# Splitting the first three units behind each normed phase by token half

## What is computed

```python
h = h + rms_norm(mix, post_mix_g[layer])
f = conv_ffn(rms_norm(h, pre_ffn_g[layer]), ffn_w_up[layer], ffn_conv_w[layer], ffn_conv_b[layer], ffn_w_down[layer])
h = h + rms_norm(f, post_ffn_g[layer])
```

## Time and profile before

| | |
|---|---|
| time, median of 3 runs | 2171.72 us (2171.62 to 2173.23) |
| span of the profiled execution | 2170.2 us |
| TensorE (PE) busy | 2142.6 us, 99% of the span |
| VectorE (DVE) busy | 1434.5 us, 66% |
| ScalarE (ACT) busy | 1015.4 us, 47% |
| DMA, mean over the span | 187 GB/s |
| chain that ended last | TensorE 96%, VectorE 1%, ScalarE 1%, issue 1% |

### The profile page before, as it was taken

The page is one execution under the profiler, slowest core; times in us unless marked ns, Lnnn a source line. Parts: engine busy times, 40 slices in busy tenths (PEclk is TensorE's granted clock), DMA queues, the critical chain, the costliest instruction groups (busy, mean ns, idle before and its releaser), DMA issues.

```text
span 2170.2 us, 32172 instructions
## 1 busy us (share of the span) xinstructions
PE 2142.6 (99%) x11234; PEld 1832.1 (84%) x11234; DVE 1434.5 (66%) x1708; ACT 1015.4 (47%) x1158; POOL 43.9 (2%) x56
## 2 busy tenths in 40 slices
PE   8999999999999999999999999999999999999998
PEld 6888878888888888888788888888888888888887
DVE  5485567878777775444765675567787877774444
ACT  5444454444444444433654574454444444444442
POOL 1030000000000000000000000000000000000000
PEclk9999999999999999999999999999999999999999
DMA  8655546666566666556455544556666666665554
GB/s 269 185 175 174 191 141 202 190 188 191 175 201 190 187 203 199 186 187 209 160 189 189 184 146 165 189 161 194 187 190 183 194 191 186 176 225 194 193 192 152
DMA packets 208226, 406.09 MB, mean 187 GB/s; under 512 B 12496, under 2 KB 12608, under 8 KB 207520
## 3 DMA queue, kind: packets, MB, share of 16 engines
q1 hardware_dynamic: 206784, 398.51, 58.5%
q0 software_dynamic: 1248, 6.67, 0.9%
q10 hardware_dynamic: 128, 0.04, 0.0%
HBM read 403.06 MB, written 2.10 MB: 187 GB/s over the span
## 4 chain that ended last, share of the span: by engine, by line
PE 96%; DVE 1%; ACT 1%; issue 1%; DMA 0%; POOL 0%; DVEq 0%; POOLq 0%; ACTq 0%; SPq 0%
PE ps L1182 37%; PE ps L1185 19%; PE ps L1198 13%; PE ps L1200 12%; PE ps L1199 12%; DVE w_lo L749 1%; PE ps L1253 1%; PE ps L1317 0%; ACT w_hi L441 0%; PE ps L1380 0%; PE ps L1351 0%; ACT x_parts L486 0%; ACT junk L478 0%; DMA h<-in_x 0%; DMA raw<-in_b_w_q 0%
## 5 line engine op out<-in xcount | busy, mean ns | idle before, releaser
L749 DVE TENSOR_TENSOR w_lo<-raw,w_hi 128x1024 fp32r<-128x1024 f32 x752 | 922.9, 1234 | 671.3 <-ACT w_hi L441 666.4
L441 ACT CAST w_hi<-raw 128x1024 fp32r<-128x1024 f32 x752 | 783.8, 1049 | 965.0 <-PE ps L1185 537.7
L1182 PE MATMUL ps<-x_parts,w_hi 128*128 128x512 f32 x3328 | 1161.5, 395 | 4.0 <-issue 2.0
L1185 PE MATMUL ps<-x_parts,w_lo 128*128 128x256 f32 x3328 | 925.2, 278 | 0.0
L1182 PEld LDWEIGHTS ps<-x_parts,w_hi 128*128 128x128 f32 x3328 | 625.7, 188 | 150.9 <-DVE w_lo L749 3.5
L1185 PEld LDWEIGHTS ps<-x_parts,w_lo 128*128 128x128 f32 x3328 | 627.1, 188 | 0.0
L1198 PE MATMUL ps<-w_hi,g_parts 128*128 128x512 f32 x704 | 273.9, 389 | 0.0
L1200 PE MATMUL ps<-w_hi,g_parts 128*128 128x512 f32 x704 | 273.9, 389 | 0.0
L1199 PE MATMUL ps<-w_lo,g_parts 128*128 128x512 f32 x704 | 273.9, 389 | 0.0
L1200 PEld LDWEIGHTS ps<-w_hi,g_parts 128*128 128x128 f32 x704 | 132.1, 188 | 27.7
L1199 PEld LDWEIGHTS ps<-w_lo,g_parts 128*128 128x128 f32 x704 | 132.1, 188 | 27.5
(11 more groups left out here) (147 smaller groups left out, 1505.2 us busy)
## 6 DMA issues: line engine op xcount, KB each, us to landing
raw<-in_ffn_w_up SPq DMA_DIRECT2D x352, 512.0 KB, 3.7
raw<-in_ffn_w_down SPq DMA_DIRECT2D x176, 512.0 KB, 4.3
raw<-in_a_w_in SPq DMA_DIRECT2D x64, 512.0 KB, 4.3
raw<-in_a_w_out SPq DMA_DIRECT2D x32, 512.0 KB, 4.2
raw<-in_b_w_q SPq DMA_DIRECT2D x32, 512.0 KB, 3.6
raw<-in_w_k SPq DMA_DIRECT2D x32, 512.0 KB, 4.1
raw<-in_w_v SPq DMA_DIRECT2D x32, 512.0 KB, 4.1
raw<-in_b_w_o SPq DMA_DIRECT2D x32, 512.0 KB, 4.5
```

Source lines behind the costliest of these rows:

```text
L441: act.copy(w_hi[:, slot, :, :], raw[:, slot, :, :]).then_inc(unit_hi, 1)
L749: dve.tensor_tensor(w_lo[:, slot, :, :], raw[:, slot, :, :], w_hi[:, slot, :, :].bitcast(F32), ALU.subtract).then_inc(unit_split, 1)
L1182: pe.matmul(ps[:, bank + m, :], w_hi[:, slot, kk, m * P:(m + 1) * P], src[:, kt, :, :].rearrange("p a t -> p (a t)"), start=first, stop=False,
L1185: mm = pe.matmul(ps[:, bank + m, 0:T], w_lo[:, slot, kk, m * P:(m + 1) * P], src[:, kt, HI, :], start=False, stop=last, skip_group_check=True)
```

## The change

The first three units behind a NORMED phase are multiplied twice: first for token half 0 alone (`early_columns(..., 0)`, L1251 of the changed kernel: eight matmuls of 256 columns, the high and low parts of 128 tokens), then for half 1 (eight such matmuls, and eight of 256 columns with `w_lo` for both halves, L1254). The six tiles of these units are transposed and split by half, in six **slots** (0 to 2 are half 0, 3 to 5 are half 1, two tiles each); tiles 6 to 15 are slots 6 to 15, whole. Slots use three PSUM banks in turn, so slot n waits until slot n-3 has been split. Slots 0 to 2 are transposed before the NORMED phase has ended. To free the banks, the last block's half 1 and the spread row move to bank 7, and half 0 to bank 2; `post_gain` moves by 8 KB in SBUF. The loops over the two pairs of a NORMED phase are written out. The orders of ScalarE and VectorE at a join are new.

```diff
+        def token_bank(ph, h_, half):
+
+            if ph in NORMED and h_:
+                return (2, 7)[half]
+            return 2 * h_ + half + (4 if ph is a_out else 0)
...
+        EARLY = 3
+        SPLIT_TILES = UK * EARLY
+
+        def slot_parts(n):
+            if n < EARLY:
+                return [(UK * n + j, 0) for j in range(UK)]
+            if n < 2 * EARLY:
+                return [(UK * (n - EARLY) + j, 1) for j in range(UK)]
+            return [(n, None)]
+
+        def slot_place(n, j):
+            bank = ps[:, 4 + n % 3, :]
+            return bank[:, j * P:(j + 1) * P] if n < 2 * EARLY else bank[:, 0:T]
+
+        def slot_tokens(half):
```

TensorE:

```diff
-                for hb in range(2):
+            def early_columns(bank, u, src, half):
+
+                tokens = slice(half * P, (half + 1) * P)
+                for m in range(TB):
+                    to = ps[:, bank + m, :].rearrange("p (a t) -> p a t", a=2)
+                    for kk in range(UK):
+                        kt = UK * u + kk
+                        pe.matmul(to[:, :, tokens], w_hi[:, u, kk, m * P:(m + 1) * P], src[:, kt, :, tokens],
+                                  start=(kt == 0 and half == 0), stop=False, skip_group_check=True)
+                        if half == NH - 1:
+                            mm = pe.matmul(ps[:, bank + m, 0:T], w_lo[:, u, kk, m * P:(m + 1) * P],
+                                           src[:, kt, HI, :], start=False, stop=False, skip_group_check=True)
+                if half == NH - 1:
+                    mm.then_inc(unit_used, 1)
+
+            def first_columns(ph, t):
+
+
+                bank = column_bank(0)
+                pe.wait_ge(evacuated, ph.block0 - 1)
+                for u in range(EARLY):
+                    pe.wait_ge(unit_hi, ph.first + u + 1)
+                    pe.wait_ge(x_ready, x_slot(t, u))
+                    early_columns(bank, u, x_parts, 0)
+                    if u:
+                        turn_slots(t, (EARLY + u - 1,))
+                for u in range(EARLY):
+                    pe.wait_ge(unit_split, ph.first + u + 1)
+                    pe.wait_ge(x_ready, x_slot(t, EARLY + u))
+                    early_columns(bank, u, x_parts, 1)
+                    turn_slots(t, ((5,), (6, 7), (8,))[u])
+                for u in range(EARLY, ph.units):
+                    slot = u % RING
+                    pe.wait_ge(unit_split, ph.first + u + 1)
+                    for m in range(TB):
+                        for kk in range(UK):
+                            kt = UK * u + kk
+                            if m == 0:
+                                pe.wait_ge(x_ready, x_whole(t, kt))
+                            pe.matmul(ps[:, bank + m, :], w_hi[:, slot, kk, m * P:(m + 1) * P],
+                                      x_parts[:, kt, :, :].rearrange("p a t -> p (a t)"), start=False, stop=False,
+                                      skip_group_check=True)
+                            mm = pe.matmul(ps[:, bank + m, 0:T], w_lo[:, slot, kk, m * P:(m + 1) * P],
+                                           x_parts[:, kt, HI, :], start=False, stop=kt == KT - 1,
+                                           skip_group_check=True)
+                        if u == EARLY and m == 1:
+                            turn_slots(t, (9,))
+                    mm.then_inc(unit_used, 1)
+                    turn_slots(t, {3: (10, 11), 4: (12, 13), 5: (14, 15)}.get(u, ()))
+                    if u == 6:
+                        spread(t)
+
...
                 mm.then_inc(half_done, 1)
                 for u in range(ph.units - RING, ph.units):
-                    tokens_out_half(ph, hb, u, 1, src, bank).then_inc(unit_used, 1)
-
-            def tokens_out(ph, i, src, ready, count, t=None):
+                    tokens_out_half(ph, hb, u, 1, src).then_inc(unit_used, 1)
+                    if t is not None and u == ph.units - 2:
+                        pe.wait_ge(evacuated, ph.block_end - 1)
+                        turn_slots(t, (0, 1))
+                if t is not None:
+                    turn_slots(t, (2,))
+
...
                     tr.then_inc(x_turned, 1)
+
+            def turn_slots(t, slots):
+                for n in slots:
+                    if n >= 3:
+                        pe.wait_ge(x_ready, x_slot(t, n - 3))
+                        if t == KV_NORM:
+                            pe.wait_ge(kv_kept, x_slot(t, n - 3) - x_base(t))
+                    for j, (k, half) in enumerate(slot_parts(n)):
+                        for a in ((0, 1) if half is None else (half,)):
+                            pe.wait_ge(h_new[a], NB * (t - 1) + k // TB + 1)
+                            c = a * P if half is None else j * P
+                            tr = pe.transpose(ps[:, 4 + n % 3, c:c + P], h[:, a, k * P:(k + 1) * P], ident[:, :])
```

ScalarE and VectorE at a join:

```diff
+                slot_high(t, (2,))
+                slot_keep(t, (0,))
+                units(ph.first, 2, 3)
+                slot_high(t, (3,))
+                slot_keep(t, (1,))
+                units(ph.first, 3, RING)
+                slot_high(t, (4,))
+                slot_keep(t, (2, 3))
+                slot_high(t, (5,))
                 units(ph.first, RING, RING + 1)
-                square_stream(t, NB - 1)
+                slot_keep(t, (4,))
+                slot_high(t, (6, 7))
+                slot_keep(t, (5, 6))
+                square_stream(t, 0)
                 units(ph.first, RING + 1, RING + 2)
-                x_high(t, range((NB - 1) * TB, KT))
-                units(ph.first, RING + 2, ph.units)
+                square_stream(t, 1)
+                slot_high(t, (8,))
+                slot_keep(t, (7,))
+                slot_high(t, (9,))
+                slot_keep(t, (8, 9))
+                square_stream(t, 2)
+                units(ph.first, RING + 2, RING + 3)
+                slot_high(t, (10, 11))
+                slot_keep(t, (10,))
+                square_stream(t, 3)
+                slot_high(t, (12,))
+                slot_keep(t, (11, 12))
+                slot_high(t, (13, 14))
+                slot_keep(t, (13, 14))
+                slot_high(t, (15,))
+                slot_keep(t, (15,))
+                units(ph.first, RING + 3, ph.units)
 
 
...
                 square(s, LAST, (0,))
-                units(nxt.first, 0, RING - 1)
+                units(nxt.first, 0, 2)
+                slot_high(s + 1, (0, 1))
...
             def turn_and_split(t, ph):
-
-
                 update_stream(t - 1, 0, 1)
+                slot_low(t, (2,))
+                update_stream(t - 1, 1, 1)
+                slot_low(t, (3,))
                 units(ph.first, 1, 2)
-                x_low(t, range(0, TB))
-                update_stream(t - 1, 1, 1)
-                units(ph.first, 2, RING - 1)
-                x_low(t, range(TB, 2 * TB))
+                slot_low(t, (4,))
+                units(ph.first, 2, 3)
+                slot_low(t, (5,))
+                slot_low(t, (6, 7))
+                units(ph.first, 3, RING)
+                update_stream(t - 1, 2, 0)
                 update_stream(t - 1, 2, 1)
-                units(ph.first, RING - 1, RING)
+                slot_low(t, (8, 9))
+                update_stream(t - 1, 3, 0)
                 update_stream(t - 1, 3, 1)
-                x_low(t, range(2 * TB, 3 * TB))
-                units(ph.first, RING, RING + 2)
+                units(ph.first, RING, RING + 1)
+                slot_low(t, (10, 11))
+                units(ph.first, RING + 1, RING + 2)
+                slot_low(t, (12, 13))
                 pre_means(t)
-                x_low(t, range(3 * TB, KT))
+                slot_low(t, (14, 15))
                 pre_diagonals(t)
                 units(ph.first, RING + 2, ph.units)
 
...
                 post_norm(s, 0)
-                for c in range(NB):
-                    update_stream(s, c, 0)
+                update_stream(s, 0, 0)
+                update_stream(s, 1, 0)
                 units(nxt.first, 0, 1)
+                slot_low(s + 1, (0, 1))
                 post_norm(s, 1)
                 turn_and_split(s + 1, nxt)
```

More of the change, by code:

```diff
@@ L290, in turned, with row_bank, x_base, x_whole @@
             return ps[:, 4 + k % 4, 0:T]
+        EARLY = 3
[10 more added lines that the diff above has]
+        def slot_tokens(half):
+            return slice(0, T) if half is None else slice(half * P, (half + 1) * P)
+        def row_bank(t):
+            return 7 if t else 4
+        def x_base(t):
+            return 0 if t == 0 else KT + (KT + SPLIT_TILES) * (t - 1)
+        def x_whole(t, k):
+            return x_base(t) + k + 1 + (SPLIT_TILES if t else 0)
+        def x_slot(t, n):
+            return x_base(t) + (UK * (n + 1) if n < 2 * EARLY else n + 1 + SPLIT_TILES)
         SCORES, SUMS, SOFTPLUS, SPLIT, WEIGHTS = 2, 5, 6, 7, 9
@@ L853, in x_low, with slot_low @@
                                              op0=ALU.mult, op1=ALU.subtract).then_inc(x_ready, 1)
```

(30 more changed lines are left out.)

111 lines of the change are left out of this document (56 added, 55 removed).

## The result

The changed kernel takes 2196.92 us (median of 4 executions: 2187.98, 2195.51, 2201.76, 2198.33) against 2172.47 us (2171.62 to 2173.36): slower by 24.5 us, about 1% (ratio 1.0100 with a 95% interval of 1.0085 to 1.0115). Forecast were 2183.7 us and a range of 2175 to 2190. The direction was right; the median lies outside the range. And there is something to notice in the four times: before spread over 2 us, after over 14.

What follows compares the result with a forecast made beforehand. TensorE, busy 99% of the span, was taken as the bound, so only its waits count. Joins would cost 28.2 us against 16.3, 12 us longer: span 2182, median 2183.7 us, range 2175 to 2190.

Steps and rivals of the forecast that it cites:

- For slot 3 0.7 us: In a join's opening, TensorE still waits 0.7 us for h of half 1 after the early half-0 work.
- for slot 8 2.0: Before tile 8's transposes, TensorE waits 2.0 us for chunk 2's updates, queued on VectorE behind slots 6 and 7.
- unit 4 1.9: Before unit 4, TensorE waits 1.9 us for `w_lo`, queued on VectorE behind slot 9 and chunk 3's updates.
- unit 6 3.1: Before unit 6, TensorE waits 3.1 us for `w_lo` behind slots 14, 15 and the diagonals; 0.9 us more at q.
- The opening: Start of each join: 1.1 us lost, where it was 3.8 to 4.3, with the full clock expected.
- the 16.3 us that the joins cost the kernel before: TensorE's loss at the three joins before the change, 16.3 us together: all the change can win.
- the added loads are hidden: At the joins, 24 more weight loads and matmuls a join were taken to cost nothing.
- The rival of 0.19 us a matmul: In split units, 256-column matmuls take 0.19 us, not 0.116; 15 us more, 2199; chance 0.03.
- The chance of 0.15 for a fall of the clock behind unit 6: Rival: the clock falls at the joins' new rests, 1.6 to 2.0 us each, 2189 with all three; chance 0.15.
- the row's 0.5 us at each join: At each join's second block, TensorE waits 0.5 us for the row copy, between nothing and 1.
- Nothing else on a path changes: Beyond the joins' terms, written-out loops and moved banks add nothing, as TensorE has no wait there.

Runs made afterwards that it cites:

- e3: The changed kernel with VectorE's split of unit 6 moved ahead of the splits of slots 14 and 15 and the diagonals; 2196.24 us, ratio 1.0098.
- e8: e4 with the row scale copied two splits earlier in the up phases and three at q; 2160.45 us, ratio 0.9938.
- e5: The changed kernel with VectorE copying the row scale one weight split earlier in the two up phases; 2188.05 us, ratio 1.0076.
- e2: The kernel before with only the three loops over pairs written out on TensorE; 2174.72 us, ratio 1.0002.
- e6: The kernel before with the row scale copied later in the two up phases, behind the second block's fourth unit's split; 2192.24 us, ratio 1.0091.
- e4: The changed kernel with new orders of slots, splits and updates at the joins on all three engines; 2184.24 us, ratio 1.0047.
- e7: e3 with the row scale copied one split earlier at all three joins; 2176.13 us, ratio 1.0010.
- e9: The changed kernel as it is, one more profiled execution; 2201.92 us.
- e11: e5's kernel unchanged, one more profiled execution; 2196.99 us.
- e12: e5's kernel unchanged, a further profiled execution; 2193.69 us.

## Why the prediction was wrong

**Right: the waits.** For slot 3 0.7 us was forecast and 0.42 came, for slot 8 2.0 and 1.23 + 0.27 = 1.5, for unit 4 1.9 and 1.7, for unit 6 3.1 and 2.8 (q 4.0 and 3.7). Each stands where VectorE's queue puts an answer behind a question, as argued. The opening kept the full clock. e3 removes the wait before unit 6 of the up joins by order alone (q keeps 0.3 us) and e8, by order again, all but those for h, and e8's gain of 13 us is in keeping with the 16.3 us that the joins cost the kernel before.

**Right: the added loads are hidden.** From the transposes at 304.86 to those at 306.99 are 2.13 us, where 0.2 + 16 x 0.116 + 0.08 = 2.14 was assumed. The rival of 0.19 us a matmul is out.

**Right in the sum, by errors that cancel.** The chance of 0.15 for a fall of the clock behind unit 6 was too low: it fell at all three joins of the profiled execution, and in 16 of the 21 such joins that the traces of this kernel and of e5's show. From unit 6 to the spread are 330.87 - 326.40 = 4.47 us against 2.86 at the full clock, 1.6 us, and at the last join more:
```profile
1464.14 0.80 PE L1283 MATMUL ps<-x_parts,w_hi 128*128 128x512 f32 x1 [2.78 <-DVE w_lo L813]
1469.43 1.02 PE L1401 MATMUL ps<-diag,ones 128*128 128x128 f32 x4
```
5.29 us, so 2.4, and as much at q. The falls cost some 6 us, about what the waits came short by (the row's 0.5 us at each join among them, 0.2 at most in these traces). The changed kernel's executions without a long stretch took 2184.21, 2184.87 and 2187.98 us as profiled, against 2183.7. That nearness is luck in part. By the terms measured here about 4 us over three joins stay unassigned in the profiled span (15.5 longer than before); the restart of TensorE behind each wait and pass is the likely place, and I didn't separate it.

**Wrong: "Nothing else on a path changes", and waits and falls of the clock priced at their own length.** I reckoned the row's copy at 0.5 us a join, "between nothing and 1", and a fall of the clock at 1.6 to 2.0 us. In these traces the copy cost 0.2 us or nothing. But the wait for it, and the return of the clock, come at the one place where the pace of the next 1344 pairs is settled: 8.9 us if it falls badly, which no term of the sum and no rival held. Of eleven executions of the changed kernel four took 2184 to 2188 us, three 2193 to 2196, one 2198 and three about 2202, with a median of 2193. These steps fit none, one or both up phases long, and q and k besides; seen in traces are three executions with none and one with both.

In the changed kernel itself the steps of the clock have at least as large a part as the wait, as far as the traces tell. Of the twelve stretches in its four traces, one has a wait there (0.18 us, long) and seven a step of the clock (one of them long). And e5's kernel, which has no wait there, still has three long stretches of nine, all three behind such a step; its eight executions have a median of 2191.6 us, not told apart from 2193. These falls follow the rest at unit 6, so the term of 3.1 us was right in its length and wrong in what it led to. The kernel before was steady, within 9 us over 31 executions, because in its up phases neither a wait nor a step of the clock stands at that place (it comes back long before the spread); only at q does a wait, of about 0.4 us, and there one trace runs short and those of e2 and e6 long, with about 3 us lost.

That the cadence is settled there, and that a wait can do it, is shown from both sides: e3's and e4's traces turn long right behind a wait with the clock at 1.00 throughout, and e7 and e8 take the waits away, and with them the long up phases and the spread. e6 brings the long one into the kernel before by moving one wait, though with a fall of the clock behind it. That a step of the clock does the same rests on the four long stretches of e9, e11 and e12, against none of 17 without either, and was not tried by itself. What tells the two cadences apart in the chip stays open, and so does why waits fell badly in 10 of 13.

## What to carry to other kernels

A wait ahead of a long, regular stream of matmuls should be priced by the stream, not by its length: look at what stands directly in front of it, and move small waits to places where transposes or another kind of matmul still follow. When a kernel's executions spread in steps, compare the number of matmuls in equal windows deep inside its phases; an engine that is 100% busy can still be 2% slower. And when work is moved ahead of a late result, list for each engine which answers now stand behind which questions; that part could be read before the run.

## What the hardware showed

- TensorE ran the same stream of 512- and 256-column matmuls at 346.3 or 352.9 ns a pair, at a granted clock of 1.00, for some 470 us without changing over.
- Behind four matmuls of 128 columns with no wait and a full clock, all 17 stretches fell into the short cadence, also where the unit just ahead of them ran in the long one (as at all three joins of e8).
- The clock fell to 0.50 behind the rests of 2.8 to 3.7 us at unit 6, but not each time: behind the seven rests of 3.7 us always, behind the fourteen of 2.8 us nine times. e5's profiled execution had the same rest of 2.78 us at the first join, and then (length, busy PE, PEclk, DMA share, GB/s)
```profile
325.95 0.50 PE L1283 MATMUL ps<-x_parts,w_hi 128*128 128x512 f32 x1 [2.78 <-DVE w_lo L813]
...
328.00:330.00 2.00, 2.00 (x14) 1.00 0.98 349
```
  The Trainium skill (TensorE: Matmul & The Clock Gate, Part 1: The HAM clock gate) has such a fall to half rate, and the trace agrees where the clock fell, at 0.50; the two cadences at one clock are a thing apart from it.
